# Scan output of a hybrid block: two pairs of heads in one PSUM bank, two sets of matmuls a group in place of four

## The reference

```python
cb = jnp.einsum('bclgn,bcsgn->bgcls', cc, bc)
y_diag = jnp.einsum('bgcls,bgrcls,bcsgrp->bclgrp', cb, decay, xdt)
...
y = y + d_skip.reshape(g, r)[..., None] * xs
yg = (y * jax.nn.silu(z.astype(jnp.float32))).reshape(b, L, g, SSD_NORM_GROUP)
yg = yg * lax.rsqrt(jnp.mean(yg * yg, -1, keepdims=True) + RMS_EPS)
```

## Time and profile before

| | |
|---|---|
| median of 3 runs | 2435.77 us |
| lowest and highest | 2435.55 and 2437.74 us |
| the profiled execution, first to last instruction | 2435.7 us |
| TensorE busy: matmuls, weight loads | 2423.8 us, 2341.2 us |
| VectorE, ScalarE, GpSimd busy | 1571.2, 1243.2, 90.5 us |
| mean granted TensorE clock | 0.999 |

### The profile page before, as it was taken

The page is one execution under the profiler, slowest core; times in us unless marked ns, Lnnn a source line. Parts: engine busy times, 40 slices in busy tenths (PEclk is TensorE's granted clock), DMA queues, the critical chain, the costliest instruction groups (busy, mean ns, idle before and its releaser), DMA issues.

```text
span 2435.7 us, 45481 instructions
## 1 busy us (share of the span) xinstructions
PE 2423.8 (100%) x19626; PEld 2341.2 (96%) x19626; DVE 1571.2 (65%) x2109; ACT 1243.2 (51%) x1426; POOL 90.5 (4%) x68
## 2 busy tenths in 40 slices
PE   9999999999999999999999999999999999999998
PEld 9999999999999999999988899999999999999998
DVE  6778878866577776666575555655655555555556
ACT  5445665554454565554464444544544445455453
POOL 0001000110021000000000000000000000000002
PEclk9999999999999999999999999999999999999999
DMA  7665656657755645546757666666555576555645
GB/s 238 198 196 180 210 180 187 185 174 236 232 175 174 199 150 165 152 150 231 232 185 244 190 203 198 187 186 197 180 190 186 190 233 208 184 171 178 188 161 182
DMA packets 267434, 467.93 MB, mean 192 GB/s; under 512 B 18955, under 2 KB 70497, under 8 KB 265313
## 3 DMA queue, kind: packets, MB, share of 16 engines
q1 hardware_dynamic: 267233, 465.02, 60.9%
HBM read 452.18 MB, written 4.26 MB: 187 GB/s over the span
## 4 chain that ended last, share of the span: by engine, by line
PE 98%; DVE 1%; ACT 0%; issue 0%; DMA 0%; SPq 0%; ACTq 0%
PE G L703 91%; PE M L703 5%; PE M L716 1%; DMA RAW<-in_ssd_w_in 0%; DVE W2m L1546 0%; DVE W0m L1546 0%; DVE E L1639 0%; ACT W0m L1125 0%; DVE E L1680 0%; DVE SZ L1708 0%; DVE E L1641 0%; ACT L1205 0%; DVE W L1546 0%; DVE W1m L1546 0%; ACT YY L1131 0%
## 5 line engine op out<-in xcount | busy, mean ns | idle before, releaser
L703 PE MATMUL G<-AA,W 128*128 128x256 f32 x7908 | 942.6, 277 | 1.1 <-DVE W L1546 1.0
L703 PEld LDWEIGHTS G<-AA,W 128*128 128x128 f32 x7908 | 917.9, 188 | 7.3 <-issue 4.1
L1546 DVE TENSOR_TENSOR W<-RAW,W 128x1024 fp32r<-128x1024 f32 x446 | 557.4, 1251 | 370.6 <-ACT W L1125 369.4
L1125 ACT CAST W<-RAW 128x1024 fp32r<-128x1024 f32 x446 | 464.8, 1047 | 467.7 <-PE G L703 457.8
L703 PE MATMUL G<-AA,WY 128*128 128x256 f32 x2508 | 305.3, 278 | 0.0
L703 PEld LDWEIGHTS G<-AA,WY 128*128 128x128 f32 x2508 | 293.2, 188 | 2.5 <-issue 2.2
L1546 DVE TENSOR_TENSOR WY<-RAW,WY 128x1024 fp32r<-128x1024 f32 (+1 forms) x112 | 140.8, 1259 | 74.9 <-ACT WY L1125 74.9
L703 PE MATMUL G<-W0m,YY 128*128 128x256 f32 x1512 | 183.8, 276 | 1.0 <-DVE W0m L1546 1.0
L703 PE MATMUL G<-W1m,YY 128*128 128x256 f32 x1512 | 182.9, 276 | 0.1
L703 PE MATMUL G<-W,YY 128*128 128x512 f32 x792 | 181.3, 389 | 0.0
L703 PE MATMUL G<-W2m,YY 128*128 128x256 f32 x1488 | 180.5, 276 | 0.0
(11 more groups left out here) (306 smaller groups left out, 2398.0 us busy)
## 6 DMA issues: line engine op xcount, KB each, us to landing
RAW<-in_a_w_in SPq DMA_DIRECT2D x192, 512.0 KB, 3.8
RAW<-in_ssd_w_in SPq DMA_DIRECT2D x160, 512.0 KB, 4.4
RAW<-in_b_w_in SPq DMA_DIRECT2D x128, 512.0 KB, 4.1
RAW<-in_dsa_w_in SPq DMA_DIRECT2D x72, 512.0 KB, 3.6
RAW<-in_ssd_w_out SPq DMA_DIRECT2D x64, 512.0 KB, 4.6
RAW<-in_dsa_w_out SPq DMA_DIRECT2D x64, 512.0 KB, 4.1
RAW<-in_a_w_out SPq DMA_DIRECT2D x64, 512.0 KB, 3.6
RAW<-in_b_w_out SPq DMA_DIRECT2D x32, 512.0 KB, 3.7
```

Of the source, the lines that this page charges most:

```text
L703: return e.matmul(o, l, r, start=start, stop=stop, skip_group_check=True)
L1125: e.copy(wh[:, 0:n], RAW[:, v % NR, 0:n]).then_inc(*up(cast_done, "cast", v))
L1546: e.tensor_tensor(wl[:, 0:n], RAW[:, v % NR, 0:n], wh[:, 0:n].bitcast(F), ALU.subtract).then_inc(*up(rest_done, "rest", v))
```

## The change

The loop over four pairs on TensorE becomes a loop over two halves of a group. In each half two pairs are done one behind the other with no unit between them; the even pair writes columns 0 to 255 of a bank, the odd one columns 256 to 511. Only the even pair's first matmul of each head has the start flag. One step of the task holds both pairs, and two `yield`s follow, so that the second half stands where the third pair stood. VectorE's four additions stay, each in its own step; the first of a half waits for both of its pairs, and the bank counts as read after the second. A group now takes six banks instead of eight. What waited for the last pair's bank to be read waits for the event "mixed_in" instead, which is counted at the same instruction.

```diff
--- before.py
+++ after.py
@@ -857,18 +857,19 @@
             yield
             yield
             yield
-            for q in range(4):
-                b = take("ty", g, q)
-                if q == 0:
+            for i in range(2):
+                b = take("ty", g, i)
+                if i == 0:
                     e.wait_ge(*on("read", "xd", g, 1))
-                if q % 2 == 0:
-                    e.wait_ge(*on("em", g, q // 2))
-                for r in range(2):
-                    h = 2 * q + r
-                    o = M[64 * r:64 * r + 64, b, :]
-                    mm(o[:, 0:256], XD[:, 0, 64 * h:64 * h + 64], E2[:, h, 0:256], True, False)
-                    last = mm(o[:, 128:256], XD[:, 1, 64 * h:64 * h + 64], E2[:, h, 256:384], False, True)
-                last.then_inc(*up(pe_made, "y_m", g, q))
+                e.wait_ge(*on("em", g, i))
+                for q in (2 * i, 2 * i + 1):
+                    for r in range(2):
+                        h = 2 * q + r
+                        o = M[64 * r:64 * r + 64, b, q % 2 * T:(q % 2 + 1) * T]
+                        mm(o[:, 0:256], XD[:, 0, 64 * h:64 * h + 64], E2[:, h, 0:256], q % 2 == 0, False)
+                        last = mm(o[:, 128:256], XD[:, 1, 64 * h:64 * h + 64], E2[:, h, 256:384], False, True)
+                last.then_inc(*up(pe_made, "y_m", g, 2 * i + 1))
+                yield
                 yield
 
         def gate_z(g):
@@ -1647,7 +1648,7 @@
             e.wait_ge(*done(b))
             if g > 1:
                 e.wait_ge(*on("y_m", g - 2, 3))
-                e.wait_ge(*on("read", "ty", g - 2, 3))
+                e.wait_ge(*on("mixed_in", g - 2, 3))
             yield from conv(b, 4 * g, XG, g_of(b))
             yield
             yield
@@ -1685,7 +1686,7 @@
                     decay(g, 1)
                     yield
             for q in range(4):
-                e.wait_ge(*on("y_m", g, q))
+                e.wait_ge(*on("y_m", g, q | 1))
                 if q == 0 and g > 0:
                     e.wait_ge(*on("yn", g - 1))
                 if q == 0 and g == 0:
@@ -1693,8 +1694,10 @@
                     e.wait_ge(*on("dtT"))
                 e.scalar_tensor_tensor(out=YT[:, q, :], in0=XG[:, q, :],
                                        scalar=dcol[:, 4 * g + q:4 * g + q + 1],
-                                       in1=M[:, bank.get(("ty", g, q), 0), 0:T], op0=ALU.mult,
-                                       op1=ALU.add).then_inc(*up(dve_made, "read", "ty", g, q))
+                                       in1=M[:, bank.get(("ty", g, q // 2), 0), q % 2 * T:(q % 2 + 1) * T],
+                                       op0=ALU.mult, op1=ALU.add).then_inc(*up(dve_made, "mixed_in", g, q))
+                if q % 2:
+                    here(dve_made, "read", "ty", g, q // 2)
                 yield
 
         def gate_z(g):
@@ -2331,7 +2334,7 @@
             for _ in range((11, 9)[g > 0]):
                 yield
             e.wait_ge(*on("g_read", ("z", g)))
-            e.wait_ge(*on("read", "ty", g, 3))
+            e.wait_ge(*on("mixed_in", g, 3))
             e.tensor_tensor(yv, yv, sz, ALU.mult).then_inc(*up(pool_made, "yz", g))
             yield
             e.wait_ge(*on("ysq", g))
```

## The result

The changed kernel takes 2429.53 us (median of 13 runs, 2428.82 to 2433.64) against 2435.55 (13 runs, 2434.77 to 2437.74) for the kernel before: 6.0 us less, a ratio of 0.9977 with a 95% interval of 0.9969 to 0.9985. A second comparison gave 2431.33 (11 runs, 2429.38 to 2433.57) against 2435.23 (22 runs), 0.9981 (0.9972 to 0.9990). So the kernel is faster, by 6.0 us by the medians of the first comparison and by 3.9 by those of the second.

The account below looks back on a forecast made before the run. TensorE's own stream was taken to bound the kernel. Fifteen joins at 0.38 give 5.7 us and the last group's first half 1.05, together 6.8, from a median of 2435.77 to 2429.0 us, range 2428.0 to 2431.9.

Parts of the forecast that it names:

- What bounds the kernel: Whole kernel: TensorE is the chain for 98% of the span, its matmuls busy 2423.8 of 2435.7 us.
- What a set costs, 1.03: Scan on TensorE: eight rows take 0.81 us as their own piece, plus 0.22 as slowness of the unit around them.
- The second set at 0.65: Joined pair in the scan: second set costs 0.65 us, one head's time, so each join saves 0.38.
- The other sum of the prediction: Scan sets: 60 cycles overhead per matmul, 0.2 us a set untouched by joining; some 3 us saved in place of 6.
- The last group: First half of the last group: second set runs inside the wait for W0m's rest, saving 1.05 us instead of 0.38.
- The sum: Whole kernel: 15 joins give 5.7 us, the last group's first half 1.05, together 6.8, so 2429.0 us.
- Edits costed at nothing: Later first unit, wait for both pairs, decays, ones sum, banks, start flags and semaphores: all taken to cost no time.
- No DMA is moved: Transfers: the change was taken to move none of them, at no cost.
- A: Joined sets: second set costs its full 0.81, only the unit's 0.22 returns; 4.2 us saved, 2431.6; chance 0.17.
- B: Last group gives nothing more than the others: 16 x 0.38 = 6.1 us, 2429.7; counted in the forecast's 0.70.
- C: Each group: second joined half waits for the decays' product on VectorE; slower, 2440.7 or more; chance 0.05.
- D: TensorE: the 0.81 piece and slow unit come back elsewhere, no change, 2435.8; chance 0.04.

Follow-up runs that it names:

- full_width: Kernel before, sets apart, but each matmul of a set has both heads' 128 weight columns instead of one head's 64: 2445.48 us against 2436.05, 1.0038.
- sets_twice: Changed kernel with each pair's matmuls done twice in a row, so four sets stand in a stretch: 2449.92 us, 1.0056.
- joined_four_banks: Order of the changed kernel with the banks of the kernel before, each pair its own: 2430.26 us against 2436.05, 0.9977.
- apart_one_bank: Banks and waits of the changed kernel with the order of the kernel before, a unit between any two sets: 2438.2 us, 1.0009.
- four_joined_sum_later: Changed kernel with four pairs in one stretch at the first half's place in groups 0 to 6, ones sum one unit later: 2475.49 us, 1.0163.
- four_late_sum_later: Changed kernel with four pairs in one stretch at the second half's place in groups 0 to 6, ones sum one unit later, heads alternating: 2443.12 us, 1.0034.

## Why the prediction was right

*What bounds the kernel.* Right, and the steadiest part of it: the first six periods of 49.82 us agree within 0.001, and in the changed kernel they shrink by what TensorE's own stream does. That "no engine else can give anything" was too much: TensorE's waits in the last group are for rests, and a transfer sent earlier by SyncE takes the wait for W1m away.

*What a set costs, 1.03, of which some 0.38 is for going to 64 columns and back.* Shown by full_width (0.05 left at full width) and sets_twice (paid once a stretch).

*The second set at 0.65.* The lower bound that I took was right for the third and fourth set and for alternating heads. As the change is written it is 0.69. The join saves 0.337 instead of 0.38: fifteen joins give 5.1 us instead of 5.7. The other sum of the prediction, with 0.2 us of a set as a fixed cost of its eight rows, which it gives as some 3 us, is 15 x 0.18 + 0.85 = 3.6 when worked out; it is excluded by the same 5.1, where it has 2.7 for the joins.

*The last group.* Forecast 1.05 for the join inside the wait and 0.38 for the other, 1.43 together; measured 24.00 − 22.73 = 1.27. Of the difference of 0.16, 0.10 is in the two units behind the wait (516.50 to the second stretch at 522.28, 5.78 where I had 5.68), 0.04 in the second join and 0.02 in the first. The rest into W2m was in time, as worked out.

*The sum.* By the traces the scan from its first set to its last ones sum went from 373.7 us to 367.7 in one profile and 368.5 in the other, 6.0 and 5.2 less where 6.8 was forecast. By the medians it is 6.0 and 3.9. The forecast of 2429.0 lay 0.5 below the first median and 2.3 below the second, both inside its range. The second is also above the 2430.9 that the prediction set for a gain that can be told from none (3.9 us against 4.9), though its interval leaves out no change. That the first came so near is partly luck: the sum was 0.8 too large by the trace, and the kernel before was 0.2 faster in that comparison than the median the forecast starts from (2435.55, 2435.77). The text on the chances says that the forecast gives up a little for a small gain, and then leaves it at 0.70.

*Edits costed at nothing.* Banks and waits: right, by joined_four_banks, which leaves out the one-bank part and loses nothing. "No DMA is moved": true of the order, and still the weak sentence of the prediction. The transfer of CSB stands in SyncE's queue behind fetches that wait for VectorE's rests, and these stand behind the group's additions, GpSimd's multiply and ScalarE's square, which moved by less than 0.1 us against the group's first set. TensorE's ones sum came earlier by the group's two joins: in group 3 the multiply ends 6.81 us ahead of it in the kernel before (337.85, 344.66) and 6.08 in the changed kernel (333.67, 339.75), and CSB goes out 1.19 us behind it (345.85) and 1.92 (341.67), 0.73 later. From the sending to the moment when VectorE is ready for it there are 9.1 to 9.4 us in the kernel before, and 8.2 to 8.5 in the groups 2 to 6 of the changed kernel; this does not shrink further from group to group. "apart_one_bank" has 8.2 to 8.3, and VectorE waits in 4 of its groups (1.3 us), though TensorE is no faster there: its additions are late instead. The lost 0.9 us or so are about what the landings had left. They cost up to 0.9 us in the last group, by chance of the landing.

The sign that the prediction named for being wrong, a wait for the rest into W1m, thus came in one profile of the changed kernel (0.94) and not in the other. The other signs held: 1.50 for a stretch (1.46 forecast), 49.15 for a group's window (49.06), no wait for E or M, and 0.24 and 0.26 us as the longest wait for W0m, where the 0.80 was.

The runs of the changed kernel scatter up to 2433.6, more than this wait explains. Six of its 24 runs have a mean granted clock of 0.998, among them the two longest of each comparison (2433.64 and 2431.38, 2433.57 and 2432.26). None of the six was profiled, so what lowers the clock in them, and what makes the difference between the two comparisons (6.0 and 3.9), was not shown.

*The rivals.* A (2431.6) is excluded by the stretch of 1.50 us, its own mark being 1.62, and by the periods; the time alone would not exclude it, since the second median is 2431.33. B's alternative for the last group didn't come; its figure, 2429.7, is within the scatter of the forecast. C did not occur in the changed kernel, and a wait of its kind did where the four sets were pushed together. D is excluded by the periods.

## What to carry to other kernels

Where matmuls with 64 weight columns are slipped in between matmuls of full width, count the changes of shape, not the matmuls: here one trip there and back costs 0.34 to 0.38 us, and an interruption at full width 0.05 (both with fp32 sets between fp32r units). Join such pieces as far as their readers and their producers allow, and stop there: four together instead of two and two should save another third of a microsecond a group (an estimate from the 0.34 of a join), but the ways to place them that were tried ran into the ones sum, the decays' product and the rests, and took 6.7 us and more above the changed kernel. When the bounding engine gets ahead by a little, look through every queue paced by another engine for a margin of the same size; a transfer that landed just in time may not any more.

## What the runs showed of the hardware

Two heads with 64 weight columns each run side by side in the array: eight rows take 0.81 us with 64 columns and 1.31 with 128, of the same form otherwise. The order in which the matmuls of the two halves are written is worth 0.04 us at the second set; the third and fourth take 0.65 each without alternating. I had not expected the order to matter.

In "four_joined_sum_later" the granted clock fell from 1.00 to 0.50 (from the 2.4 to the 1.2 GHz level) in a wait of TensorE of 5.7 us, and it still was 0.50 in the 4 us behind it, where two sets take 2.85 us instead of 1.50. A longer wait for VectorE thus costs more than its own length, which is part of the 2475 us of that kernel. A shorter one can do it too: behind the 2.9 us for W1m in "four_late_sum_later" the next 2.4 us have a mean of 0.70. At the start of the kernel, behind waits of 1.2 and 1.0 us, it fell to 0.50 in the first profile of the kernel before, and not in the first of the changed kernel behind a wait of 1.0.
